# A hybrid encoder block: the first four MLP units in two token halves, and GpSimd scaling part of three tiles

## The chip, the cores and the metric

The kernel runs on one NeuronCore of a Trainium2 chip. The metric is the device time of one execution in microseconds (us); lower is better. Engines: TensorE (PE in the profile), VectorE (DVE), ScalarE (ACT), GpSimd (POOL), and SyncE (SP), which issues the weight loads.

## What is computed

512 tokens of width 2048 in float32: an adaLN-modulated token-mixing layer of two parallel attention groups, an output projection, a residual, then an adaLN-modulated squared-ReLU MLP of width 8192. The change sits at the seam between the two:

```python
o = o @ w_out[l]
x = x + gt_a * rms_norm(o, g_post_attn[l])
h = rms_norm(x, g_pre_mlp[l]) * (1.0 + sc_m) + sh_m
y = jnp.square(jax.nn.relu(h @ w_mlp_in[l])) @ w_mlp_out[l]
x = x + gt_m * rms_norm(y, g_post_mlp[l])
```

## The kernel before

All programs are written out by hand, one per engine; semaphores tie them together, and each engine runs its instructions strictly in the order written. Float32 products are made of three passes: every operand is split into a high part (rounded, fp32r) and a low part (the rest), and TensorE adds high x high, high x low and low x high. For a weight, ScalarE copies the landed block `raw` to `hi` (`split_hi`, 128x1024) and VectorE subtracts to get `lo` (`split_lo`). A *unit* is one such block of 256 rows of a weight matrix, a ring of four of them is in flight.

The 512 tokens are four tiles t = 0 to 3 of 128 on the partitions. The last column block of the output projection runs tile by tile, so that the tiles finish one after another (`b_tile`, `w_used`). For each tile:

- VectorE adds the two attention groups' parts (`sum_tile`, L1742) and gates them (`gate_tile`, L1747), ScalarE squares (`square_last`, L1086, into PSUM bank 2 or 3 as scratch, hence `row_done` before the MLP may use these banks), VectorE and ScalarE make the factor (`z_variance`, `root`), VectorE adds the residual in two halves of 1024 columns (`residual`, L1793, both inputs in SBUF).
- ScalarE squares the result in two halves (L1107); one tile later `x1_variance`, `root`, `x1_factor` (L1778) give the second norm's factor `rstd`, semaphore `x1_rstd`.
- The tile is scaled by it into `z_tok`: columns 0 to 511 (`xn_ready`) and 512 to 2047 (`xn_rest`), on ScalarE for tiles 0 to 2 (L1090) and on VectorE for tile 3 (L1813).

Then TensorE transposes z_tok in blocks of 128x128 (L2466): four blocks make column block k (0 to 15) of all 512 tokens in one PSUM bank. ScalarE and VectorE turn it into h2 = x*gsc_m + shf_m (printed as h_f, h_hi, h_lo, whose memory it shares): for even k ScalarE makes both the float32 and the high part (L1117, L1118), for odd k VectorE makes the float32 part (L1819) and ScalarE copies it to the high part (L1121); VectorE subtracts for the low part (L1824). `h2_mid`, `h2_hi_done` and `h2_ready` count these.

MLP unit j needs column blocks k = 2j and 2j+1 and is 24 matmuls of 512 columns. `first_columns` does unit 0, `up_block` units 1 to 7, with `before_first` putting the transposes of four more blocks ahead of units 1, 3 and 5. Splits of units 1 to 5 stand among the h2 instructions (`FIRST_AFTER`).

GpSimd does nothing at the seam: its last instructions ahead of it are the loads of bias rows, and then it waits to store the MLP's results.

Of the kernel before, what the change touches and what calls it, by code (L numbers as in the profile page):

```python
# [193 lines left out]
def build(nc, a, out, x1_dram, y_dram):  # L194
    with ExitStack() as ctx:
# [525 lines left out]
        def _(act):  # L721
# [369 lines left out]

            for t in range(NT):
# [11 lines left out]
                for half in range(2):  # L1104
                    act.wait_ge(x1_ready, 2 * t + half + 1)
                    cols = slice(half * HALF, (half + 1) * HALF)
                    nc.scalar.activation(z_tok[:, t, cols], x_res[:, t, cols], ACT.Square, accum_out=stat[:, t, 1 + half:2 + half]).then_inc(x1_sq, 1)  # L1107
                act.dma_start(x1_d[t], x_res[:, t, :]).then_inc(x1_saved, 16)
# [2 lines left out]
            for k in range(KD):
                if k % 2 == 0:
                    src, g, b = bank[4 + k % 4][:], gsc_m[:, k:k + 1], shf_m[:, k:k + 1]
                    act.wait_ge(xn_turned, k + 1)
                    if k >= 4:
                        act.wait_ge(h2_ready, k - 3)
                    nc.scalar.activation(h2_f32[k % 4][:], src, ACT.Identity, scale=g, bias=b)  # L1117
                    nc.scalar.activation(h2_hi[:, k, :], src, ACT.Identity, scale=g, bias=b).then_inc(h2_hi_done, 1)  # L1118
                else:
                    act.wait_ge(h2_mid, k // 2 + 1)  # L1120
                    nc.scalar.activation(h2_hi[:, k, :], h2_f32[k % 4][:], ACT.Copy).then_inc(h2_hi_done, 1)  # L1121
                for j in FIRST_AFTER.get(k, ()):
                    split_hi(*at_mlp(0, j))
# [109 lines left out]
        def _(dve):  # L1233
# [578 lines left out]
            for cols, ready in ((slice(0, COLS), xn_ready), (slice(COLS, D), xn_rest)):  # L1812
                ts(z_tok[:, NT - 1, cols], x_res[:, NT - 1, cols], rstd[:, NT - 1, 1:2], None, ALU.mult).then_inc(ready, 1)  # L1813
            for k in range(KD):
                if k % 2 == 0:

                    dve.wait_ge(xn_turned, k + 2)
                    k1 = k + 1
                    ts(h2_f32[k1 % 4][:], bank[4 + k1 % 4][:], gsc_m[:, k1:k1 + 1], shf_m[:, k1:k1 + 1],  # L1819
                       ALU.mult, ALU.add).then_inc(h2_mid, 1)  # L1820
                else:
                    dve.wait_ge(h2_mid, k // 2 + 1)
                dve.wait_ge(h2_hi_done, k + 1)
                tt(h2_lo[:, k, :], h2_f32[k % 4][:], h2_hi[:, k, :].bitcast(F32), ALU.subtract).then_inc(h2_ready, 1)  # L1824
                for j in FIRST_AFTER.get(k, ()):
                    split_lo(*at_mlp(0, j))
# [231 lines left out]
        def _(pe):  # L2058
# [406 lines left out]
            def turn_x1(k, t, out_bank):  # L2465
                return nc.tensor.transpose(out_bank[:, t * P:(t + 1) * P], z_tok[:, t, k * P:(k + 1) * P], ident[:])  # L2466

            pe.wait_ge(b_sum, 4 * NB)
            for t in range(NT):
                pe.wait_ge(xn_ready, t + 1)  # L2470
                for k in range(4):
                    ins = turn_x1(k, t, bank[4 + k])
                    if t == NT - 1:
                        ins.then_inc(xn_turned, 1)
            pe.wait_ge(row_done, 4 * NB)


            def first_columns():
# [3 lines left out]
                pe.wait_ge(raw_used, at_mlp(0, 0)[0].count(1, 1))
                pe.wait_ge(h2_hi_done, 1)
                for n in range(4):
                    mm(bank[n][:], hi[s][:, 0, n * P:(n + 1) * P], h2_hi[:, 0, :], start=True, stop=False)
                    mm(bank[n][:], lo[s][:, 0, n * P:(n + 1) * P], h2_hi[:, 0, :], start=False, stop=False)
                pe.wait_ge(h2_ready, 1)
                for n in range(4):
                    mm(bank[n][:], hi[s][:, 0, n * P:(n + 1) * P], h2_lo[:, 0, :], start=False, stop=False)
                pe.wait_ge(h2_ready, 2)  # L2490
                for n in range(4):
                    wh, wl = hi[s][:, 1, n * P:(n + 1) * P], lo[s][:, 1, n * P:(n + 1) * P]
                    mm(bank[n][:], wh, h2_hi[:, 1, :], start=False, stop=False)
                    mm(bank[n][:], wh, h2_lo[:, 1, :], start=False, stop=False)
                    ins = mm(bank[n][:], wl, h2_hi[:, 1, :], start=False, stop=False)
                ins.then_inc(w_used, 1)
# [30 lines left out]

            def before_first(j):


                if j in (1, 3, 5):
                    pe.wait_ge(h2_ready, 2 * j + 2)
                    pe.wait_ge(xn_rest, NT)
                    for k in range(2 * j + 2, 2 * j + 6):
                        for t in range(NT):
                            ins = turn_x1(k, t, bank[4 + k % 4])
                        ins.then_inc(xn_turned, 1)
                pe.wait_ge(h2_ready, 2 * j + 2)

            first_columns()  # L2540
            up_block(0, 0, before_first, range(1, UNITS_D))
            pe.wait_ge(h2_ready, KD)
# [206 lines left out]
```

## Time and profile before

| | us |
|---|---|
| median of 3 runs | 2118.05 (2114.66 to 2118.88) |
| the profiled execution's own time | 2119.17 |
| its span, first to last instruction | 2117.5 |
| TensorE busy | 2068.4 |
| VectorE, ScalarE, GpSimd busy | 1493.1, 844.1, 150.0 |

Times in the views are us from the span's start. In a timeline row stand start, duration, engine, line, operation, tiles written and read, and in brackets how long the engine was idle before it and what ended that.

### The profile page before, as it was taken

The numbers are of one execution on the slowest core, as the hardware profiler recorded it, in microseconds if no ns is written. First come the engines' busy times: TensorE is split into PE (matmuls) and PEld (weight loads), VectorE is DVE, ScalarE is ACT, GpSimd is POOL, SyncE is SP. The second block draws the span as 40 slices with busy tenths as digits, with TensorE's granted clock in tenths as the row PEclk, the third lists the DMA queues.
The fourth block names the chain that finished last, engine by engine and source line by source line (L and its number), as shares of the span: only waits on it lengthen the run. The fifth ranks groups of instructions, "written<-read, shape, count | busy, mean of one in ns | idle before, by whom it ended". The sixth has DMA issues, their size and how long they took to land.

```text
span 2117.5 us, 26317 instructions
## 1 busy us (share of the span) xinstructions
PE 2068.4 (98%) x9370; PEld 1710.2 (81%) x9370; DVE 1493.1 (71%) x1797; ACT 844.1 (40%) x1153; POOL 150.0 (7%) x159
## 2 busy tenths in 40 slices
PE   7999999999999989999999999999999999999998
PEld 6887888887788878888888888888788888888886
DVE  5876898788877776445544454434889888888866
ACT  4444322588733363233322332233333333333422
POOL 0000000038700000000000000012000000000000
PEclk9999999999999999999999999999999999999999
DMA  9986869600287736655665566666767456456442
GB/s 310 323 296 216 276 210 250 199 30 11 68 280 234 254 128 228 222 187 188 222 235 187 188 204 224 216 229 219 252 235 262 136 215 260 150 207 238 178 179 80
DMA packets 214353, 435.20 MB, mean 206 GB/s; under 512 B 30180, under 2 KB 69768, under 8 KB 205448
## 3 DMA queue, kind: packets, MB, share of 16 engines
q1 hardware_dynamic: 196136, 361.43, 50.8%
q0 software_dynamic: 16704, 67.11, 8.9%
q10 hardware_dynamic: 1440, 5.70, 0.7%
q8 instruction: 44, 0.72, 0.1%
q14 instruction: 29, 0.24, 0.0%
HBM read 367.09 MB, written 67.11 MB: 205 GB/s over the span
## 4 chain that ended last, share of the span: by engine, by line
PE 81%; DVE 6%; DMA 5%; issue 3%; ACT 3%; POOL 2%; SPq 0%; DVEq 0%; ACTq 0%; POOLq 0%
PE bank L2085 10%; PE bank L2087 10%; PE bank L2086 10%; PE bank L2523 7%; PE bank L2525 7%; PE bank L2524 7%; PE bank L2072 6%; PE bank L2074 6%; PE bank L2073 6%; DMA y_dram<-y_out 1%; DMA rows<-in_g_post_mlp 1%; PE bank L2574 1%; PE bank L2573 1%; PE bank L2572 1%; DMA w<-in_w_mlp_out 1%
## 5 line engine op out<-in xcount | busy, mean ns | idle before, releaser
L1241 DVE TENSOR_TENSOR lo<-raw,hi 128x1024 fp32r<-128x1024 f32 (+2 forms) x234 | 275.7, 1182 | 375.1 <-ACT hi L728 373.0
L728 ACT ACTIVATE hi<-raw 128x1024 fp32r<-128x1024 f32 (+2 forms) x236 | 239.5, 1023 | 655.4 <-PE bank L2087 410.9
L2085 PE MATMUL bank<-h_hi,hi 128*128 128x512 f32 x1016 | 396.0, 390 | 0.0
L2087 PE MATMUL bank<-h_hi,lo 128*128 128x512 f32 x1016 | 395.3, 389 | 0.0
L2086 PE MATMUL bank<-h_lo,hi 128*128 128x512 f32 x1016 | 395.3, 389 | 0.0
L2523 PE MATMUL bank<-hi,y_use 128*128 128x512 f32 x784 | 307.0, 392 | 7.3 <-DVE acc L1968 3.8
L2525 PE MATMUL bank<-hi,y_use 128*128 128x512 f32 x784 | 305.8, 390 | 0.0
L2524 PE MATMUL bank<-lo,y_use 128*128 128x512 f32 x784 | 305.7, 390 | 0.0
L1184 ACT ACTIVATE hi<-w 128x1024 fp32r<-128x1024 f32 x168 | 178.2, 1062 | 295.5 <-PE bank L2525 221.8
L1892 DVE TENSOR_TENSOR lo<-w,hi 128x1024 fp32r<-128x1024 f32 x168 | 204.7, 1223 | 37.5 <-ACT hi L1184 36.8
L2085 PEld LDWEIGHTS bank<-h_hi,hi 128*128 128x128 f32 x1016 | 190.7, 188 | 40.1 <-issue 0.7
L2087 PEld LDWEIGHTS bank<-h_hi,lo 128*128 128x128 f32 x1016 | 190.7, 188 | 39.7
L2086 PEld LDWEIGHTS bank<-h_lo,hi 128*128 128x128 f32 x1016 | 190.7, 188 | 39.5 <-issue 0.2
L2523 PEld LDWEIGHTS bank<-hi,y_use 128*128 128x128 f32 x784 | 147.5, 188 | 43.1 <-issue 12.7
L2525 PEld LDWEIGHTS bank<-hi,y_use 128*128 128x128 f32 x784 | 147.5, 188 | 30.8
L2524 PEld LDWEIGHTS bank<-lo,y_use 128*128 128x128 f32 x784 | 147.5, 188 | 30.3
L2072 PE MATMUL bank<-hi,h_hi 128*128 128x512 f32 x320 | 125.9, 394 | 1.4 <-ACT q_o L886 1.4
L2074 PE MATMUL bank<-hi,h_lo 128*128 128x512 f32 x320 | 124.7, 390 | 0.0
L2073 PE MATMUL bank<-lo,h_hi 128*128 128x512 f32 x320 | 124.5, 389 | 0.0
L1968 DVE TENSOR_TENSOR acc<-bank,acc 128x1024 f32<-128x1024 f32 x84 | 102.5, 1220 | 0.0
L2072 PE MATMUL bank<-hi,o_hi 128*128 128x512 f32 x224 | 89.3, 399 | 0.1
L2074 PE MATMUL bank<-hi,o_lo 128*128 128x512 f32 x224 | 88.0, 393 | 0.0
(318 smaller groups left out, 3124.9 us busy)
## 6 DMA issues: line engine op xcount, KB each, us to landing
raw<-in_w_ada SPq DMA_DIRECT2D x192, 512.0 KB, 5.1
raw<-in_w_mlp_in SPq DMA_DIRECT2D x128, 512.0 KB, 4.3
w<-in_w_mlp_out SPq DMA_DIRECT2D x128, 512.0 KB, 5.2
y_dram<-y_out POOLq DMA_DIRECT2D x32, 1792.0 KB, 7.8
y_use<-y_dram SPq DMA_DIRECT2D x53, 1024.0 KB, 8.8
raw<-in_w_in SPq DMA_DIRECT2D x32, 512.0 KB, 5.4
raw<-in_w_out SPq DMA_DIRECT2D x32, 512.0 KB, 4.7
raw<-in_w_in SPq DMA_DIRECT2D x48, 256.0 KB, 5.8
```

Source lines behind the costliest of these rows:

```text
L728: ins = nc.scalar.activation(dst, src, ACT.Copy)
L1241: ins = tt(dst, src, high.bitcast(F32), ALU.subtract)
L1892: tt(lo[w.slot()][:], weight(np, i, h)[:], hi[w.slot()][:].bitcast(F32), ALU.subtract).then_inc(dn_lo, 1)
L2072: mm(acc[t][:], xh, hi[s][:, q, :], start=first and q == 0, stop=False)
L2073: mm(acc[t][:], xh, lo[s][:, q, :], start=False, stop=False)
L2074: ins = mm(acc[t][:], xl, hi[s][:, q, :], start=False, stop=last and q == QROWS - 1)
L2085: mm(acc[n][:], wh, act_hi[:, k, :], start=first and q == 0, stop=False)
L2086: mm(acc[n][:], wh, act_lo[:, k, :], start=False, stop=False)
L2087: ins = mm(acc[n][:], wl, act_hi[:, k, :], start=False, stop=last and q == QROWS - 1)
L2523: mm(bank[b + m][:], yh, hi[s][:, q, :], start=j == 0, stop=False)
L2524: mm(bank[b + m][:], yh, lo[s][:, q, :], start=False, stop=False)
L2525: ins = mm(bank[b + m][:], yl, hi[s][:, q, :], start=False, stop=j == PAIRS - 1)
```

## The change

TensorE's first four MLP units are done in two passes, first on tokens 0 to 255 (tiles 0 and 1) and later on tokens 256 to 511, each with 24 matmuls of 256 columns. To that end column blocks k = 0 to 7 are turned and made into h2 in halves too: `TURNED` lists 24 pieces i: 0 to 7 are blocks 0 to 7 of the first half, 8 to 15 the same blocks of the second half, 16 to 23 blocks 8 to 15 whole. The first three pieces are transposed between the projection's last matmuls of tile 3, and the h2 instructions of the first pieces and the splits of units 0 to 3 are placed among the steps of tiles 2 and 3 on ScalarE and VectorE. The scaling of columns 512 to 2047 of tiles 0 to 2 goes from ScalarE to GpSimd.

```diff
+FIRST_K = KD // 2
+TURNED = [(k, half) for half in range(2) for k in range(FIRST_K)] + [(k, None) for k in range(FIRST_K, KD)]
...
+        def turned_at(i):
+            k, half = TURNED[i]
+            if half is None:
+                return k, slice(0, T), bank[4 + i % 4][:], h2_f32[i % 4][:]
+            cols = slice(half * HALF_T, (half + 1) * HALF_T)
+            return k, cols, bank[4 + i % 4][:, 0:HALF_T], h2_half[i % 4][:]
...
+            def h2_high(i):
+                k, cols, src, mid = turned_at(i)
+                dst, g, b = h2_hi[:, k, cols], gsc_m[:, k:k + 1], shf_m[:, k:k + 1]
+                if i % 2 == 0:
+                    act.wait_ge(xn_turned, i + 1)
...
+                    nc.scalar.activation(dst, src, ACT.Identity, scale=g, bias=b).then_inc(h2_hi_done, 1)
+                    nc.scalar.activation(mid, src, ACT.Identity, scale=g, bias=b).then_inc(h2_mid, 1)
+                else:
+                    act.wait_ge(h2_mid, i + 1)
+                    nc.scalar.activation(dst, mid, ACT.Copy).then_inc(h2_hi_done, 1)
             for t in range(NT):
                 square_last(t)
                 if t:
                     root(2 * t, t - 1, 1)
+                if t == 3:
+                    split_hi(*at_mlp(0, 1))
                 root(2 * t + 1, t, 0)
                 if t:
                     act.wait_ge(x1_rstd, t)
                     scale_x1(t - 1, slice(0, COLS), xn_ready)
-                    if t < NT - 1:
-                        scale_x1(t - 1, slice(COLS, D), xn_rest)
-                    else:
-                        split_hi(*at_mlp(0, 0))
...
+                if t == 2:
+                    split_hi(*at_mlp(0, 0))
+                if t == 3:
+                    h2_high(2)
+                    h2_high(3)
+                x1_square(t, 0)
+                if t == 2:
+                    h2_high(0)
+                x1_square(t, 1)
+                if t == 2:
+                    h2_high(1)
+            split_hi(*at_mlp(0, 2))
             root(2 * NT, NT - 1, 1)
-            scale_x1(NT - 2, slice(COLS, D), xn_rest)
...
+            def h2_two(i):
+                h2_middle(i + 1)
+                h2_low(i)
+                h2_low(i + 1)
             for t in range(NT):
                 if t < NT - 1:
                     dve.wait_ge(b_tile, t + 1)
                 else:
+                    split_lo(*at_mlp(0, 0))
+                    h2_two(0)
                     dve.wait_ge(w_used, MLP_W)
                 sum_tile(NB - 1, t)
                 gate_tile(NB - 1, t)
                 if t:
                     x1_variance(t - 1)
+                if t == NT - 1:
+                    split_lo(*at_mlp(0, 1))
                 z_variance(t)
                 if t:
                     x1_factor(t - 1)
+                if t == NT - 1:
+                    h2_two(2)
                 residual(t)
-            split_lo(*at_mlp(0, 0))
+            split_lo(*at_mlp(0, 2))
             x1_variance(NT - 1)
+            h2_two(4)
             x1_factor(NT - 1)
...
+                    if t == NT - 1 and j == 6:
+                        pe.wait_ge(xn_ready, 2)
+                        pe.wait_ge(b_sum, 4 * (NB - 1) + 3)
+                        for i in range(3):
+                            turn_x1(i)
...
+            def first_columns(half, j):
...
+                for q in range(QROWS):
+                    k = QROWS * j + q
+                    i = FIRST_K * half + k
+                    pe.wait_ge(h2_hi_done, i + 1)
+                    for n in range(4):
+                        mm(bank[n][:, cols], hi[s][:, q, n * P:(n + 1) * P], h2_hi[:, k, cols], start=k == 0 and half == 0, stop=False)
+                        mm(bank[n][:, cols], lo[s][:, q, n * P:(n + 1) * P], h2_hi[:, k, cols], start=False, stop=False)
+                    pe.wait_ge(h2_ready, i + 1)
+                    for n in range(4):
+                        ins = mm(bank[n][:, cols], hi[s][:, q, n * P:(n + 1) * P], h2_lo[:, k, cols], start=False, stop=False)
...
+            pe.wait_ge(row_done, 4 * NB)
+            first_columns(0, 0)
+            pe.wait_ge(b_sum, 4 * NB)
+            turn_more(3, 4, 5)
+            first_columns(0, 1)
+            turn_more(6, 7)
+            first_columns(0, 2)
+            first_columns(0, 3)
+            turn_more(8, 9, 10, 11)
+            for j in range(FIRST_K // QROWS):
+                first_columns(1, j)
+                turn_more(12 + 2 * j, 13 + 2 * j)
+            up_block(0, 0, before_first, range(FIRST_K // QROWS, UNITS_D))
...
+            for t in range(NT - 1):
+                pool.wait_ge(x1_rstd, t + 1)
+                nc.gpsimd.tensor_scalar(z_tok[:, t, COLS:D], x_res[:, t, COLS:D], rstd[:, t, 1:2], None, ALU.mult).then_inc(xn_rest, 1)
```

`turn_more` transposes the pieces it is given, with the waits that free their banks. How the orders move at two places:

VectorE from the residual of tile 2 to that of tile 3, before (L1793 is the residual, L1742 and L1747 sum and gate of tile 3):

```order
L1793 SCALAR_TENSOR_TENSOR x_res<-z_tok,rstd,x_res 128x1024 x2
L1742 SCALAR_TENSOR_TENSOR part<-bank,r_out,part 128x512
L1747 TENSOR_TENSOR z_tok<-part,comb 128x512
L1772 TENSOR_TENSOR stat<-stat 128x1
L1773 TENSOR_SCALAR stat_v<-stat 128x1
L1783 TENSOR_REDUCE stat<-row_sq 128x1
L1784 TENSOR_SCALAR stat_v<-stat 128x1
L1778 RECIPROCAL rstd<-stat_s 128x1
L1789 RECIPROCAL rstd<-stat_s 128x1
L1793 SCALAR_TENSOR_TENSOR x_res<-z_tok,rstd,x_res 128x1024 x2
```

The same place after (L1827 is the residual, L1776 the sum, L1275 `split_lo`, L1836 `h2_middle`, L1843 `h2_low`), first from the residual of tile 2 to the gate of tile 3:

```order
L1827 SCALAR_TENSOR_TENSOR x_res<-z_tok,rstd,x_res 128x1024 x2
L1275 TENSOR_TENSOR lo_85<-raw_73,hi_81 128x1024
L1836 TENSOR_SCALAR h_half_164<-bank,gsc_m,shf_m 128x256
L1843 TENSOR_TENSOR h_lo<-h_half_163,h_hi 128x256
L1843 TENSOR_TENSOR h_lo<-h_half_164,h_hi 128x256
L1776 SCALAR_TENSOR_TENSOR part<-bank,r_out,part 128x512
L1781 TENSOR_TENSOR z_tok<-part,comb 128x512
```

and from there to the residual of tile 3:

```order
L1275 TENSOR_TENSOR lo_86<-raw_74,hi_82 128x1024
L1817 TENSOR_REDUCE stat<-row_sq 128x1
L1818 TENSOR_SCALAR stat_v<-stat 128x1
L1812 RECIPROCAL rstd<-stat_s 128x1
L1836 TENSOR_SCALAR h_half_166<-bank,gsc_m,shf_m 128x256
L1843 TENSOR_TENSOR h_lo<-h_half_165,h_hi 128x256
L1843 TENSOR_TENSOR h_lo<-h_half_166,h_hi 128x256
L1823 RECIPROCAL rstd<-stat_s 128x1
L1827 SCALAR_TENSOR_TENSOR x_res<-z_tok,rstd,x_res 128x1024 x2
```

Four instructions have moved ahead of tile 3's sum, and four more stand between its gate and its residual.

ScalarE behind `square_last` of tile 3 up to the first h2 piece of unit 2's columns, after (L739 `split_hi`, L1088 `root`, L1101 the scaling, L1107 the squares of tile 3, L1121, L1122 and L1125 `h2_high`):

```order
L1088 ACTIVATE stat_s<-stat_v 128x1
L739 ACTIVATE hi_82<-raw_74 128x1024
L1088 ACTIVATE stat_s<-stat_v 128x1
L1101 ACTIVATE z_tok<-x_res,rstd 128x512
L1121 ACTIVATE h_hi<-bank,shf_m,gsc_m 128x256
L1122 ACTIVATE h_half_165<-bank,shf_m,gsc_m 128x256
L1125 ACTIVATE h_hi<-h_half_166 128x256
L1107 ACTIVATE z_tok,stat<-x_res 128x1024 x2
L1109 DMA x_dram<-x_res 128x2048
L739 ACTIVATE hi_83<-raw_75 128x1024
L1088 ACTIVATE stat_s<-stat_v 128x1
L1121 ACTIVATE h_hi<-bank,shf_m,gsc_m 128x256
```

Before, only the two roots, one scaling and one `split_hi` stood between `square_last` and the squares of tile 3, and the h2 instructions all came behind. L1109 is the store of the tile, which both kernels have.

## Rows read from the trace of the kernel before

**Rows 1.** The page: engines' busy us (share of span), chain by engine.

```profile
PE 2068.4 (98%) x9370; PEld 1710.2 (81%) x9370; DVE 1493.1 (71%) x1797; ACT 844.1 (40%) x1153; POOL 150.0 (7%) x159
...
PE 81%; DVE 6%; DMA 5%; issue 3%; ACT 3%; POOL 2%; SPq 0%; DVEq 0%; ACTq 0%; POOLq 0%
```

**Rows 2.** Waits of TensorE: who for whom, us, times, longest.

```profile
PE bank L2466 <- DVE z_tok L1813: 3.9, 1, 3.9
...
PE bank L2485 <- ACT h_hi L1118: 1.1, 1, 1.1
PE bank L2466 <- DVE part L1742: 1.0, 1, 1.0
PE bank L2466 <- ACT z_tok L1090: 0.9, 1, 0.9
```

**Rows 3.** Timeline, TensorE, 757 to 778.

```profile
757.63 0.39 PE L2449 MATMUL bank<-lo,o_hi 128*128 128x512 f32 x1
757.86 0.39 PE L2450 MATMUL bank<-hi,o_lo 128*128 128x512 f32 x1
...
768.00 0.77 PE L2485 MATMUL bank<-h_hi,hi 128*128 128x512 f32 x1 [1.05 <-ACT h_hi L1118]
...
772.86 0.40 PE L2493 MATMUL bank<-h_hi,hi 128*128 128x512 f32 x1
...
775.61 1.91 PE L2466 MATMUL bank<-ident,z_tok 128*128 128x128 f32 x16
777.27 0.47 PE L2085 MATMUL bank<-h_hi,hi 128*128 128x512 f32 x1
```

**Rows 4.** Windows: us, PE busy, PEclk, DMA share, GB/s.

```profile
764.00:766.00 2.00, 0.17 (x1) 0.89 0.98 393
...
771.00:772.00 1.00, 1.00 (x4) 0.50 0.06 16
772.00:773.00 1.00, 1.00 (x5) 0.81 0.00 0
```

**Rows 5.** Timeline, VectorE, 758 to 764.

```profile
758.29 0.75 DVE L1742 SCALAR_TENSOR_TENSOR part<-bank,r_out,part 128x512 f32<-128x512 f32 x1 [0.46 <-PE bank L2450]
...
760.78 2.48 DVE L1793 SCALAR_TENSOR_TENSOR x_res<-z_tok,rstd,x_res 128x1024 f32<-128x1024 f32 x2
```

**Rows 6.** Timeline, TensorE at 739.94; then line L2087's weight loads.

```profile
739.94 1.84 PE L2459 MATMUL bank<-ones,mod_acc 128*128 128x1 f32 x16
...
L2087 PEld LDWEIGHTS bank<-h_hi,lo x1016: 187/188/188, 777.6 to 1474.9; 128*128 128x128 f32 x170
```

**Rows 7.** Groups of ScalarE and VectorE, 741 to 775, and L1843.

```profile
L1090 ACT ACTIVATE z_tok<-x_res,rstd 128x1536 f32<-128x1536 f32 x3 | 4.7, 1566 | 0.0
...
L1090 ACT ACTIVATE z_tok<-x_res,rstd 128x512 f32<-128x512 f32 x3 | 2.2, 724 | 0.0
...
L1824 DVE TENSOR_TENSOR h_lo<-h_f,h_hi 128x512 fp32r<-128x512 f32 x4 | 2.7, 688 | 0.6 <-ACT h_hi L1118 0.5 <-ACT h_hi L1121 0.2
...
L1843 DVE TENSOR_TENSOR y_mix<-y_mix x28: 424/426/426, 823.7 to 1396.7; 128x256 f32<-128x256 f32 x28
```

**Rows 8.** Groups of GpSimd by form: busy, mean ns, idle.

```profile
L2611 POOL TENSOR_TENSOR sq_sum<-sq_sum,sq 128x512 f32<-128x512 f32 x15 | 20.1, 1341 | 31.4 <-ACT sq L975 31.4
...
L2623 POOL CAST q_hi<-q_o 128x512 fp32r<-128x512 f32 x10 | 6.3, 630 | 281.9 <-PE bank L2306 281.9
...
L2648 POOL MEMSET sq_sum<- 128x1024 f32 x1 | 1.0, 957 | 7.1 <-PE bank L2366 7.1
```

**Rows 9.** Timeline, all engines, 549 to 551; then line L1629.

```profile
549.16 1.48 POOL L2611 TENSOR_TENSOR sq_sum<-sq_sum,sq 128x512 f32<-128x512 f32 x1
...
549.40 1.78 DVE L1629 TENSOR_TENSOR lo<-raw,hi 128x512 fp32r<-128x512 f32 x1
...
550.58 1.08 POOL L2643 CAST v_hi<-v_lat 128x512 fp32r<-128x512 f32 x1
...
L1629 DVE TENSOR_TENSOR lo<-raw,hi x4: 680/701/1785, 518.1 to 554.9; 128x512 fp32r<-128x512 f32 x4
```

More of the change, by code:

```diff
@@ L122 @@
 MLP_RAW_END = MLP_RAW_LAST + MLP_N
-FIRST_AFTER = {3: [1], 7: [2, 3], 11: [4, 5]}
 FIRST_SPLIT = 6
+FIRST_K = KD // 2
+TURNED = [(k, half) for half in range(2) for k in range(FIRST_K)] + [(k, None) for k in range(FIRST_K, KD)]
+TURNED_N = len(TURNED)
 PAIRS = FCH // 2
@@ L294, in build @@
         h2_f32 = [sb(f"h2_f32_{i}", 188 + 2 * i, [T]) for i in range(4)]
+        h2_half = [sb(f"h2_half_{i}", 188 + i, [HALF_T]) for i in range(4)]
         y_mix = sb("y_mix", 116, [SLOTS + 1, HALF_T])
@@ L1090, in scale_x1, with x1_square @@
                 nc.scalar.activation(z_tok[:, t, cols], x_res[:, t, cols], ACT.Copy, scale=rstd[:, t, 1:2]).then_inc(ready, 1)
+            def x1_square(t, half):
+                act.wait_ge(x1_ready, 2 * t + half + 1)
+                cols = slice(half * HALF, (half + 1) * HALF)
+                nc.scalar.activation(z_tok[:, t, cols], x_res[:, t, cols], ACT.Square, accum_out=stat[:, t, 1 + half:2 + half]).then_inc(x1_sq, 1)
+                if half:
+                    act.dma_start(x1_d[t], x_res[:, t, :]).then_inc(x1_saved, 16)
+            def h2_high(i):
[3 more added lines that the diff above has]
+                    act.wait_ge(xn_turned, i + 1)
+                    if i >= 2 * FIRST_K:
+                        act.wait_ge(h2_ready, max(2 * FIRST_K, i - 3))
+                    elif i >= 4:
+                        act.wait_ge(h2_ready, i - 3)
+                    nc.scalar.activation(dst, src, ACT.Identity, scale=g, bias=b).then_inc(h2_hi_done, 1)
[3 more added lines that the diff above has]
+                    nc.scalar.activation(dst, mid, ACT.Copy).then_inc(h2_hi_done, 1)
             for t in range(NT):
@@ L1099, in _ @@
                     scale_x1(t - 1, slice(0, COLS), xn_ready)
-                    if t < NT - 1:
-                        scale_x1(t - 1, slice(COLS, D), xn_rest)
-                    else:
-                        split_hi(*at_mlp(0, 0))
[L1104 to L1108, printed above, removed]
-            root(2 * NT, NT - 1, 1)
-            scale_x1(NT - 2, slice(COLS, D), xn_rest)
[L1111 to L1123, printed above, removed]
+                if t == 2:
[10 more added lines that the diff above has]
+            split_hi(*at_mlp(0, 2))
+            root(2 * NT, NT - 1, 1)
+            for i in range(4, 2 * FIRST_K):
+                h2_high(i)
+                if i == 5:
+                    split_hi(*at_mlp(0, 3))
+            for i in range(2 * FIRST_K, TURNED_N):
+                h2_high(i)
+                if i in (2 * FIRST_K + 1, 2 * FIRST_K + 5):
+                    split_hi(*at_mlp(0, 4 + (i - 2 * FIRST_K) // 4))
             def relu_pair(g, f, pr):
@@ L1793, in residual, with h2_middle, h2_low @@
                     stt(x_res[:, t, cols], z_tok[:, t, cols], rstd[:, t, 0:1], x_res[:, t, cols], ALU.mult, ALU.add).then_inc(x1_ready, 1)
+            def h2_middle(i):
+                k, _, src, mid = turned_at(i)
+                dve.wait_ge(xn_turned, i + 1)
+                if i >= 4:
+                    dve.wait_ge(h2_hi_done, i - 3)
+                dve.wait_ge(h2_mid, i)
+                ts(mid, src, gsc_m[:, k:k + 1], shf_m[:, k:k + 1], ALU.mult, ALU.add).then_inc(h2_mid, 1)
+            def h2_low(i):
+                k, cols, _, mid = turned_at(i)
+                dve.wait_ge(h2_mid, i + 1)
+                dve.wait_ge(h2_hi_done, i + 1)
+                tt(h2_lo[:, k, cols], mid, h2_hi[:, k, cols].bitcast(F32), ALU.subtract).then_inc(h2_ready, 1)
+            def h2_two(i):
+                h2_middle(i + 1)
+                h2_low(i)
+                h2_low(i + 1)
             for t in range(NT):
@@ L1806, in _ @@
                     x1_factor(t - 1)
+                if t == NT - 1:
+                    h2_two(2)
                 residual(t)
-            split_lo(*at_mlp(0, 0))
+            split_lo(*at_mlp(0, 2))
             x1_variance(NT - 1)
+            h2_two(4)
             x1_factor(NT - 1)
             dve.wait_ge(x1_rstd, NT)
[L1812 to L1826, printed above, removed]
+            ts(z_tok[:, NT - 1, 0:COLS], x_res[:, NT - 1, 0:COLS], rstd[:, NT - 1, 1:2], None, ALU.mult).then_inc(xn_ready, 1)
+            split_lo(*at_mlp(0, 3))
+            h2_two(6)
+            ts(z_tok[:, NT - 1, COLS:D], x_res[:, NT - 1, COLS:D], rstd[:, NT - 1, 1:2], None, ALU.mult).then_inc(xn_rest, 1)
+            for i in range(FIRST_K, TURNED_N, 2):
+                h2_two(i)
+                if i in (2 * FIRST_K, 2 * FIRST_K + 4):
+                    split_lo(*at_mlp(0, 4 + (i - 2 * FIRST_K) // 4))
             def mix_pair(g, f, pr):
@@ L2431, in out_block, with turn_x1 @@
                         spread_ga(n)
+            def turn_x1(i):
+                k, half = TURNED[i]
+                _, _, dst, _ = turned_at(i)
+                tiles = range(NT) if half is None else (2 * half, 2 * half + 1)
+                for m, t in enumerate(tiles):
+                    ins = nc.tensor.transpose(dst[:, m * P:(m + 1) * P], z_tok[:, t, k * P:(k + 1) * P], ident[:])
+                ins.then_inc(xn_turned, 1)
             out_block(0, first=True)
@@ L2463, in _ @@
             pe.wait_ge(mod_read, MODS + 4)
[L2465 to L2474, printed above, removed]
@@ L2475, in _ @@
-            pe.wait_ge(row_done, 4 * NB)
-            def first_columns():
-                w = at_mlp(0, 0)[1]
-                s = w.slot()
[L2482 to L2496, printed above, removed]
+            def first_columns(half, j):
+                r, w = at_mlp(0, j)
+                s = w.slot()
+                cols = slice(half * HALF_T, (half + 1) * HALF_T)
+                pe.wait_ge(raw_used, r.count(1, 1))
+                for q in range(QROWS):
[8 more added lines that the diff above has]
+                        ins = mm(bank[n][:, cols], hi[s][:, q, n * P:(n + 1) * P], h2_lo[:, k, cols], start=False, stop=False)
+                if half:
+                    ins.then_inc(w_used, 1)
@@ L2526, in dn_products, with turn_more @@
                         ins.then_inc(w_used, 1)
-            def before_first(j):
[L2531 to L2542, printed above, removed]
+            def turn_more(*which):
+                for i in which:
+                    if i == 4:
+                        pe.wait_ge(xn_rest, 2)
+                    if i == FIRST_K:
+                        pe.wait_ge(xn_ready, NT)
+                    if i == FIRST_K + 4:
+                        pe.wait_ge(xn_rest, NT)
+                    if i >= 4:
+                        pe.wait_ge(h2_ready, i - 3)
+                    turn_x1(i)
+            def before_first(j):
+                pe.wait_ge(h2_ready, FIRST_K + 2 * j + 2)
+                if j < UNITS_D - 2:
+                    turn_more(FIRST_K + 2 * j + 4, FIRST_K + 2 * j + 5)
+            pe.wait_ge(row_done, 4 * NB)
[11 more added lines that the diff above has]
+            up_block(0, 0, before_first, range(FIRST_K // QROWS, UNITS_D))
+            pe.wait_ge(h2_ready, TURNED_N)
             up_block(0, 1)
```

## The prediction

> **What bounds the kernel now.** The page first: TensorE (PE) is busy 98% of the span and holds 81% of the chain that ended last [rows 1]. So an edit on another engine pays only where TensorE waits. The list of its waits shows four at the seam between output projection and MLP: 3.9, 1.1, 1.0 and 0.9 us, 6.9 us together [rows 2]. The timeline places them: the last projection matmul starts at 757.86, the first MLP matmul at 768.00 [rows 3]; between them stand 16 transposes. The clock adds to that: after TensorE's idle stretch the granted clock falls in 764 to 766 from 1.00 (2.4 GHz) to 0.50 (1.2 GHz) and is back in 772 to 773 [rows 4]; twelve matmuls run from 768.00 to 772.86, 4.9 us, where the dense rate (starts 0.227 apart, 757.63 and 757.86 [rows 3]) gives 2.7. So 2.2 us go to the clock. From 777.27, where unit 1 starts, TensorE does not wait before the end of the first MLP half [rows 3]. What happens behind 777.27 is then a sum of TensorE work: whatever the change delays there is paid in full, as the rest of the up phase is dense.
>
> What is late at the seam is tile 3: VectorE's sum of tile 3 starts at 758.29 (L1742), its residual at 760.78 (L1793) and takes 2.48 for two halves [rows 5], then ScalarE squares, root, factor, z_tok, transposes, h2. That chain is serial.
>
> **The change, walked.** I put down for each engine its instructions in program order and let each start at the later of two times: the end of the one ahead of it, or 0.03 us after the last instruction that it waits for. Full-size durations are from rows; where instructions follow back to back I take the spacing of their starts in the timeline, which is some 0.08 less than a recorded duration. The same walk over the order of before puts unit 1 at 777.2 against 777.27 in the trace, so the method is good to about 0.3 us.
>
> New prices. *256-column matmul:* none in the trace. Half of 0.227 is 0.113; if the 0.0135 us by which 0.227 exceeds 512 columns at 2.4 GHz stays whole, it is 0.120. I take 0.120. A weight load is recorded as 0.188 [rows 6], and could be the floor; but sixteen one-column matmuls with their loads take 1.84 us, 0.105 apart [rows 6], so loads do overlap and I keep 0.188 as the upper bound only. *ScalarE on 256 columns:* 1024 columns fewer save 0.84 (1.566 against 0.724) [rows 7], so 256 fewer save 0.21: 0.45 from PSUM, 0.30 from SBUF. *VectorE on 256:* 0.42 against 0.69 for 512 [rows 7], starts 0.34 apart. *GpSimd on 1536 columns:* not in the trace. MEMSET of 1024 takes 0.96 and a CAST of 512 0.63 [rows 8]; CAST plus 1024 columns at MEMSET's rate is 1.6 at most, and MEMSET's rate over 1536 alone 1.4: 1.5, taken. CAST three times over gives 1.9; three two-input operations of 1.3 (L2611) give 3.9, the upper end.
>
> *GpSimd's new work holds VectorE.* At 549.40 a VectorE subtraction of 512 columns with both inputs in SBUF took 1.78 while GpSimd's L2611 ran from 549.16 to 550.64; its least is 0.68 [rows 9]. 1.78 is just the rest of GpSimd's instruction plus its own 0.6. The residual (z_tok and x_res) is such an instruction, and GpSimd's scaling of tile t is released by the very factor (x1_rstd) that stands 0.2 us ahead of the residual of tile t+1 on VectorE. So each scaling of 1.5 holds a residual by about 1.25, at tile 1 and at tile 2. The Trainium skill (GPSIMD Engine Reference, Key points) names the same sharing, for VectorE instructions with two SBUF inputs or in a 2-port mode; the trace agrees with 1.78 against 0.68. It speaks against this change: what ScalarE saves per tile (1.566, L1090 [rows 7]) lay beside the residual anyway.
>
> The walk, us from the span's start:
> - Residual 1, ready at 749.8, is held and ends 753.5; sum 2 follows at once; residual 2 is ready at 756.15, is held and ends 758.6.
> - Now VectorE does, ahead of sum 3, split_lo of unit 0, one middle and two lows of 256 columns, the last of which waits for ScalarE's square of tile 2 and copy: sum 3 starts at 762.5, before 758.29. 4.2 us late.
> - ScalarE's square_last(3) ends 763.85, so TensorE (row_done) starts its first half-matmuls at 764.0: 4.0 us *earlier* than before, after 5.3 us idle. This is the gain.
> - Before residual 3 stand split_lo of unit 1, factor 2, a middle and two lows, each pair handed over to ScalarE and back. Residual 3 runs 770.4 to 772.8; before 760.78 to 763.26. 9.6 us late.
> - Squares of tile 3 end 773.9, split_hi of unit 2 774.9, split_lo 776.2, root 776.7, h2 of k = 4 on ScalarE 777.2. TensorE, which ran dry at 772.6, starts unit 2's first half at 777.5. By then it has done 48 half-matmuls, the work of one whole unit, and 16 transposes.
>
> At that same time (777.27) before has done one whole unit and 32 transposes. So the early start buys nothing, and from here on the two are compared as sums:
> - start later: 777.5 against 777.3, +0.3 rounded up
> - 16 transposes more to do; sixteen take 1.66 from the start of the first to unit 1's start [rows 3]: +1.7
> - 144 half-matmuls still to come in place of 72 full ones: 144 x 0.120 - 72 x 0.227 = +0.95
> - clock: with about 5 us idle before 777.5, more than the 3.9 us wait in which it fell before [rows 2, 4], I expect 0.50 for some 4 us of work again, as from 768.00 to 772.4. Some 16 to 20 half-matmuls at 0.213 (256 columns at 1.2 GHz) instead of 0.120, part of it in waits anyway: +1.6. The half clock of before lies ahead of 777.27 and is in the comparison already; that of the first burst (764) hides behind the wait for tile 3.
> - new waits: h2 of k = 0 second half 0.1 and 0.4, split_lo of units 4 and 5 0.3 each: +1.1
>
> Sum +5.7 us. VectorE's own waits, the x1 stores and the POOL queue (its row loads are issued ahead of the scaling, and its first save waits for the first MLP half) lie beside TensorE work and cost nothing; units 6 to 8 are split 1 to 2 us later than before while TensorE needs them 5 later, so no weight is late. The profiled execution took 2119.17 with a span of 2117.5; the median of the runs is 2118.05, 1.1 lower, within their spread. A difference carries over: **2118.05 + 5.7 = 2123.7 us**, 0.27% slower. A measurement of this kernel tells about 0.2%, 4.2 us, from no change.
>
> The Trainium skill (TensorE: Matmul & The Clock Gate, Back-to-back issue gap) gives 262 cycles for 256 columns and 518 for 512, 109 and 216 ns at 2.4 GHz. The trace has 227 for 512, so the measurement decides. By the page's gap the sum would be 1.6 lower, +4.1.
>
> **Rivals.**
> 1. *No hold by GpSimd.* If its scaling fits between VectorE's instructions, or is done before the residual, both residuals keep their times: sum 3 starts at 760.4, TensorE at 761.9, unit 2 at 775.2, and the walk ends 2.3 (clock full) to 3.3 us later than before: about 2121, inside 0.2%. For it: GpSimd itself stretches too (a CAST took 1.08 at 550.58 [rows 9], beside VectorE, against its mean of 0.63), so the two may share. Against: 1.78.
> 2. *GpSimd at the two-input rate*, 3.9 us a tile: each residual held 3.65; the walk ends 10.8 later, 2128.9. For: its rate for a scalar from memory is not shown. Against: the one-input CAST.
> 3. *Weight load as floor.* With 0.13 per half-matmul +1.2 on the sum, with 0.15 +3.6, with 0.188 +8.4 (2132). Against: 0.105 apart.
> 4. *The second hole closes, and it is faster.* All rests on unit 2's first half starting when TensorE is free. If tile 3's residual kept its old place, as when VectorE takes sum 3 and residual 3 by 764 and the h2 halves are served in their gaps, TensorE would go from 762 without a stop: 48 half-matmuls 5.8 and 16 transposes 1.7 end at 769.5 instead of 777.5, no half clock behind. 5.7 - 8 - 1.6 = -3.9, 2114. It decides from unit 2 starting before 769. Against: in the program's order VectorE can't reach sum 3 before the low of the second h2 half, and residual 3 stands behind ScalarE's copy. Little chance.
> 5. *The change does not start TensorE early*: first half-matmul at 768 or later, e.g. a hold longer than I think. Then everything behind shifts by what it is over 764 less the slack of the burst; it falls in with 2.
>
> **How the numbers follow.** Main case 0.43, rival 1 0.28, rival 2 (with 5) 0.12, rival 3 0.08, rival 4 0.05, and 0.04 for an end within 0.2% that no case here has. The main case spreads from under 4.2 (half-matmuls at 0.113, a clock that is back sooner) to above 7. Of the main case's 0.43 I put 0.06 under 4.2. Slower 0.37 + 0.12 + 0.08 = 0.57, same 0.28 + 0.06 + 0.04 = 0.38, faster 0.05. The range 2117.5 to 2129.0 takes in rival 1 with room below and rival 2, and leaves out rival 4 and most of rival 3.
>
> **What would show it.** Right: first half-matmul at 762 to 764.5, residual halves of tiles 1 and 2 at 2.5 instead of 1.28 while GpSimd runs, residual 3 at 768 to 771, a TensorE wait of about 5 us ahead of unit 2, clock 0.50 after it, 256-column matmuls 0.11 to 0.12 apart. Wrong: no such wait, or residuals at 1.28, or half-matmuls 0.15 apart and more, or TensorE waiting later in the up phase for weights.

## The result and the profile after

The changed kernel takes **2131.11 us** (median of 5, 2128.32 to 2133.55), before in the same runs 2118.88 (2114.66 to 2119.55). The ratio is 1.0058, 95% interval 1.0047 to 1.0069: slower by 12.2 us at the medians. Forecast were 2123.7 and at most 2129.0. The direction held, the size did not.

The profiled execution took 2133.55 with a span of 2131.9, 14.4 over that of before. To see where these 14.4 lie I cut both traces at two events that both have: the start of the residual of tile 1 on VectorE, and the last matmul of the up phase on TensorE. In the kernel before these stand at 749.87 and 1475.15; I call the 725.28 between them *the stretch*. After, from the timelines of VectorE (cut at 753, so only the first of the two halves is in the row) and TensorE:

```profile
751.59 4.18 DVE L1827 SCALAR_TENSOR_TENSOR x_res<-z_tok,rstd,x_res 128x1024 f32<-128x1024 f32 x1
...
1487.61 0.39 PE L2143 MATMUL bank<-h_hi,lo 128*128 128x512 f32 x1
```

The stretch is now 736.02, **+10.7**. Ahead of it stand +1.7: in this execution the granted clock over 20 to 50 us was 0.77 (before's profile 0.89), and kernels made from either one (below) show one value or the other: 0.77 in e2, e3 and e7, 0.89 in e1, e4, e5, e6 and e8. So I take it for no effect of the change. Behind the stretch stand +1.9 (644.29 to the span's end against 642.35), of which 1.0 is a longer wait for the first weights of the down phase. What the change did is thus looked for in the stretch, and below every kernel is compared by it too. For comparison with before, 1.72 is to be taken off the times of after.

The waits of TensorE at the seam, in place of [rows 2]:

```profile
PE bank L2546 <- ACT bank L1097: 7.0, 1, 7.0
...
PE bank L2546 <- ACT h_hi L1121: 4.9, 1, 4.9
...
PE bank L2495 <- ACT z_tok L1101: 1.4, 1, 1.4
```

13.3 us where before had 6.9. The cause can be read from GpSimd and VectorE. GpSimd's timeline, and VectorE's, with the residuals of tiles 1 and 2:

```profile
751.41 4.17 POOL L2756 TENSOR_SCALAR z_tok<-x_res,rstd 128x1536 f32<-128x1536 f32 x1 [39.41 <-DVE rstd L1812]
759.31 4.16 POOL L2756 TENSOR_SCALAR z_tok<-x_res,rstd 128x1536 f32<-128x1536 f32 x1 [3.74 <-DVE rstd L1812]
772.14 4.17 POOL L2756 TENSOR_SCALAR z_tok<-x_res,rstd 128x1536 f32<-128x1536 f32 x1 [8.66 <-DVE rstd L1812]
```

```profile
751.59 5.38 DVE L1827 SCALAR_TENSOR_TENSOR x_res<-z_tok,rstd,x_res 128x1024 f32<-128x1024 f32 x2
756.89 0.74 DVE L1776 SCALAR_TENSOR_TENSOR part<-bank,r_out,part 128x512 f32<-128x512 f32 x1
...
759.62 5.26 DVE L1827 SCALAR_TENSOR_TENSOR x_res<-z_tok,rstd,x_res 128x1024 f32<-128x1024 f32 x2
764.80 1.21 DVE L1275 TENSOR_TENSOR lo<-raw,hi 128x1024 fp32r<-128x1024 f32 x1
...
767.56 0.74 DVE L1776 SCALAR_TENSOR_TENSOR part<-bank,r_out,part 128x512 f32<-128x512 f32 x1
```

The scaling takes 4.17 us, where 1.5 was forecast. The residuals take 5.38 and 5.26 in place of 2.48 [rows 5], and only the first half of each pair is long: 4.18 at tile 1. They are thus held by 2.9 and 2.8 us. Sum 3 (L1776) starts at 767.56. On TensorE that arrives as:

```profile
769.26 0.55 PE L2546 MATMUL bank<-h_hi,hi 128*128 128x256 f32 x1 [6.95 <-ACT bank L1097]
...
783.37 0.55 PE L2546 MATMUL bank<-h_hi,hi 128*128 128x256 f32 x1 [4.89 <-ACT h_hi L1121]
```

The windows around both waits (columns as in [rows 4]):

```profile
764.00:766.00 2.00, 0.00 (x0) 1.00 0.16 66
...
770.00:774.00 4.00, 4.00 (x21) 0.50 0.28 74
774.00:776.00 2.00, 2.00 (x19) 0.97 0.43 163
...
784.00:787.00 3.00, 3.00 (x16) 0.50 0.36 134
787.00:789.00 2.00, 2.00 (x16) 0.80 0.44 74
```

TensorE goes to half clock twice: after 7 idle us, and again after 4.9.

### The profile page after: what moved, and what is told of

Same layout as the page of the kernel before. It is cut to its first block, busy times and chain, and to the rows that moved or that the text cites. A ratio compares the mean times of both kernels' runs of the same rounds, so it can differ in the third digit from the quotient of the medians.

```text
span 2131.9 us, 26571 instructions
## 1 busy us (share of the span) xinstructions
PE 2073.4 (97%) x9466; PEld 1719.1 (81%) x9466; DVE 1499.8 (70%) x1809; ACT 843.4 (40%) x1162; POOL 162.7 (8%) x162
## 4 chain that ended last, share of the span: by engine, by line
PE 84%; DVE 6%; ACT 3%; issue 3%; DMA 2%; POOL 1%; SPq 0%; DVEq 0%; ACTq 0%; POOLq 0%
PE bank L2141 11%; PE bank L2142 11%; PE bank L2143 11%; PE bank L2579 7%; PE bank L2581 7%; PE bank L2580 7%; PE bank L2128 6%; PE bank L2129 6%; PE bank L2130 6%; PE bank L2647 1%; PE bank L2646 1%; PE bank L2648 1%; PE bank L2200 1%; PE bank L2202 1%; PE bank L2201 1%
## 5 line engine op out<-in xcount | busy, mean ns | idle before, releaser
L1275 DVE TENSOR_TENSOR lo<-raw,hi 128x1024 fp32r<-128x1024 f32 (+2 forms) x234 | 275.6, 1181 | 381.0 <-ACT hi L739 378.9
L739 ACT ACTIVATE hi<-raw 128x1024 fp32r<-128x1024 f32 (+2 forms) x236 | 239.8, 1023 | 658.4 <-PE bank L2143 411.5
L2141 PE MATMUL bank<-h_hi,hi 128*128 128x512 f32 x992 | 386.6, 390 | 0.5 <-DVE lo L1275 0.5
L2142 PE MATMUL bank<-h_lo,hi 128*128 128x512 f32 x992 | 385.9, 389 | 0.0
L2143 PE MATMUL bank<-h_hi,lo 128*128 128x512 f32 x992 | 385.9, 389 | 0.0
L2141 PEld LDWEIGHTS bank<-h_hi,hi 128*128 128x128 f32 x992 | 186.2, 188 | 39.9 <-DVE lo L1275 1.0
L2142 PEld LDWEIGHTS bank<-h_lo,hi 128*128 128x128 f32 x992 | 186.2, 188 | 38.8 <-issue 0.2
L2143 PEld LDWEIGHTS bank<-h_hi,lo 128*128 128x128 f32 x992 | 186.2, 188 | 38.7
L2129 PE MATMUL bank<-lo,o_hi 128*128 128x512 f32 x224 | 87.9, 393 | 0.0
```

Source lines behind the costliest of these rows:

```text
L739: ins = nc.scalar.activation(dst, src, ACT.Copy)
L1275: ins = tt(dst, src, high.bitcast(F32), ALU.subtract)
L2129: mm(acc[t][:], xh, lo[s][:, q, :], start=False, stop=False)
L2141: mm(acc[n][:], wh, act_hi[:, k, :], start=first and q == 0, stop=False)
L2142: mm(acc[n][:], wh, act_lo[:, k, :], start=False, stop=False)
L2143: ins = mm(acc[n][:], wl, act_hi[:, k, :], start=False, stop=last and q == QROWS - 1)
```

## The experiments

Two causes stood against each other at the start. **The hold:** GpSimd's instruction keeps VectorE from starting a residual, and that is more than half of the loss. **The halves:** the loss is in the new order and its extra small work, whoever scales. Each kernel is told with its median and ratio (95% interval), and with its stretch against the 725.28 of before. Runs of before beside e1 to e4 have the median 2118.79, beside e5 to e7 2119.2, beside e8 2119.15.

**e1_scale_on_act.** The halves stay; ScalarE scales the rest of tiles 0 to 2 again, in its idle places.

```
         if t == 1:
+            scale_x1(0, slice(COLS, D), xn_rest)
...
             split_hi(*at_mlp(0, 1))
+            scale_x1(1, slice(COLS, D), xn_rest)
...
             h2_high(3)
+            scale_x1(2, slice(COLS, D), xn_rest)
...
-    nc.gpsimd.tensor_scalar(z_tok[:, t, COLS:D], x_res[:, t, COLS:D], rstd[:, t, 1:2], None, ALU.mult)
```

> The changed kernel with one part undone: columns 512 to 2047 of tiles 0 to 2 are scaled on ScalarE again, in places where it idles in the changed kernel; GpSimd has no work at the seam. Theory A (GpSimd's 4.17 us instruction holds VectorE's residual): the residual halves of tiles 1 and 2 take 2.48 together again instead of 5.38 and 5.26, sum 3 comes 5 us earlier, and the kernel is 6 to 8 us faster than the changed one, 2123 to 2125 us, still 3 to 6 slower than the one before, since tile 3's chain stands behind h2 pieces and splits. Rival B (the loss is the late place of tile 3's chain and the half clock alone, the hold being covered by waits that come anyway): under 2 us faster than the changed one, about 2130.

2124.42 us, ratio 1.0027 (1.0018 to 1.0036), stretch +4.3. Its residual of tile 1, and its two TensorE starts:

```profile
749.71 2.48 DVE L1831 SCALAR_TENSOR_TENSOR x_res<-z_tok,rstd,x_res 128x1024 f32<-128x1024 f32 x2
```

```profile
762.07 0.51 PE L2550 MATMUL bank<-h_hi,hi 128*128 128x256 f32 x1 [3.29 <-ACT bank L1097]
...
775.52 0.36 PE L2550 MATMUL bank<-h_hi,hi 128*128 128x256 f32 x1 [4.89 <-ACT h_hi L1121]
```

The time is in the expected range. The hold is gone, and with it 6.5 of the stretch's 10.7. That is a little more than the two holds (5.7). The rest, 4.3, belongs to the halves and their order: the second wait is still 4.9 us.

**e2_before_gpsimd.** The other part alone: the kernel before, with only the rest scaling of tiles 0 to 2 moved to GpSimd.

```
-    scale_x1(t - 1, slice(COLS, D), xn_rest)
...
-scale_x1(NT - 2, slice(COLS, D), xn_rest)
...
+for t in range(NT - 1):
+    pool.wait_ge(x1_rstd, t + 1)
+    nc.gpsimd.tensor_scalar(z_tok[:, t, COLS:D], x_res[:, t, COLS:D], rstd[:, t, 1:2], None, ALU.mult).then_inc(xn_rest, 1)
```

> The kernel before with one part of the change alone: GpSimd scales columns 512 to 2047 of tiles 0 to 2, all else as before, full-width units. Theory A: the residuals of tiles 1 and 2 are held some 2.8 us each, sum 3 comes near 763 instead of 758.3, TensorE's wait grows by 5, and with a longer half clock the kernel is 5 to 7 us slower than before, 2124 to 2126. Rival B: within 1 us of before.

2127.73 us, ratio 1.0038 (1.0025 to 1.0051), stretch +8.5: more than expected. In this order the third scaling meets a residual as well (764.34 on GpSimd, 764.64 on VectorE), so three are held:

```profile
748.72 5.38 DVE L1790 SCALAR_TENSOR_TENSOR x_res<-z_tok,rstd,x_res 128x1024 f32<-128x1024 f32 x2
...
756.74 5.25 DVE L1790 SCALAR_TENSOR_TENSOR x_res<-z_tok,rstd,x_res 128x1024 f32<-128x1024 f32 x2
764.64 5.25 DVE L1790 SCALAR_TENSOR_TENSOR x_res<-z_tok,rstd,x_res 128x1024 f32<-128x1024 f32 x2
```

Counted from the start of residual 1, residual 3 ends 7.8 later than before, and the other 0.7 comes from a longer half clock behind it (from the first MLP matmul to unit 1's start 10.0 us, for 9.3). So GpSimd alone makes before slower, without any halves.

**e3_gpsimd_pieces.** The changed kernel, with each scaling of 1536 columns issued as three of 512.

```
-    nc.gpsimd.tensor_scalar(z_tok[:, t, COLS:D], x_res[:, t, COLS:D], ...).then_inc(xn_rest, 1)
+    for n in range(1, NB):
+        cols = slice(n * COLS, (n + 1) * COLS)
+        ins = nc.gpsimd.tensor_scalar(z_tok[:, t, cols], x_res[:, t, cols], rstd[:, t, 1:2], None, ALU.mult)
+    ins.then_inc(xn_rest, 1)
```

> The changed kernel with each of GpSimd's three instructions of 1536 columns cut into three of 512. Theory A, hold for the length of one instruction: a residual half waits for the piece under way only, about 1 us, the two halves of a tile take 3.5 to 4.5 us instead of 5.3, and the kernel is 2 to 4 us faster than the changed one, 2127 to 2129. Rival C (the two engines share SBUF bandwidth and VectorE is slowed in proportion to the bytes GpSimd moves): the same bytes cost the same, residuals 5.3, no change, 2131.

2125.38 us, ratio 1.0031 (1.002 to 1.0042), stretch +5.2. GpSimd works longer than before, and VectorE is held less:

```profile
750.92 4.83 POOL L2758 TENSOR_SCALAR z_tok<-x_res,rstd 128x512 f32<-128x512 f32 x3 [39.03 <-DVE rstd L1812]
756.66 5.88 POOL L2758 TENSOR_SCALAR z_tok<-x_res,rstd 128x512 f32<-128x512 f32 x3 [0.91 <-DVE rstd L1812]
```

```profile
751.11 3.21 DVE L1827 SCALAR_TENSOR_TENSOR x_res<-z_tok,rstd,x_res 128x1024 f32<-128x1024 f32 x2
756.96 3.09 DVE L1827 SCALAR_TENSOR_TENSOR x_res<-z_tok,rstd,x_res 128x1024 f32<-128x1024 f32 x2
```

The holds are 0.7 and 0.6, less than expected (3.5 to 4.5 for two halves), and the kernel is faster than the hold theory had put it (2127 to 2129). Both halves of residual 1 are held, each for a little: 1.58 and 1.71 in place of 1.28. So what counts here is not GpSimd's total time but how long one instruction of it is: VectorE gets its turn near the end of each.

**e4_keep_busy.** The changed kernel, with identity transposes in TensorE's two waits: 55 ahead of unit 0 and 44 ahead of the transposes of k = 6 and 7. It prices the clock.

```
+def keep_busy(n, b):
+    for _ in range(n):
+        nc.tensor.transpose(bank[b][:, 0:P], ident[:], ident[:])
...
+keep_busy(55, 0)
 pe.wait_ge(row_done, 4 * NB)
...
+pe.wait_ge(h2_ready, 3)
+keep_busy(44, 6)
 turn_more(6, 7)
```

> The changed kernel with TensorE doing 55 transposes of the identity in its first wait and 44 in its second, into PSUM space that is free then; nothing else differs. If the half clock behind the two waits costs what the sum says: granted clock 1.00 throughout, the burst at 783 runs at 0.12 per half-matmul from its start, the kernel is 2 to 3 us faster than the changed one, about 2129 (the first burst's half clock being hidden behind tile 3's chain). If the half clock costs nothing because waits end it all: no change. If the added transposes are themselves in the way: slower.

2127.92 us, ratio 1.0049 (1.0035 to 1.0062), stretch +9.4. That is 1.3 less than after in the stretch, and 3.1 less by the medians, each against its own before; the expected 2 to 3 us are in the time and not in the stretch. The granted clock is 1.00 in every window of the seam:

```profile
784.00:787.00 3.00, 2.79 (x23) 1.00 0.28 46
```

Behind unit 2's start the stretch is 1.1 shorter (703.14 for 704.24). Ahead of it next to nothing is gained, though the transposes behind unit 0 come 2.3 sooner. VectorE's float32 part of piece 3 starts 0.9 sooner (22.26 after residual 1's start, for 23.19), but the two lows behind it now meet GpSimd's third scaling (770.51 to 774.67):

```profile
772.21 0.54 DVE L1836 TENSOR_SCALAR h_half<-bank,gsc_m,shf_m 128x256 f32<-128x256 f32 x1 [1.79 <-ACT h_half L1122]
772.67 1.74 DVE L1843 TENSOR_TENSOR h_lo<-h_half,h_hi 128x256 fp32r<-128x256 f32 x2
```

They end at 774.4, where ScalarE's copy for the second one is done by 773.2. So e4 prices the clock behind unit 2, and the clock ahead of it only mixed with a new hold. Most of the loss stands without the half clock.

**e5_reordered.** What is left after e1 should be the lateness of tile 3. This kernel has the halves, no GpSimd work, and another order of steps on two engines. VectorE's piece around tile 3 (S sum and gate, X and F variance and factor of x, Z variance of z, R residual, s split, w a pair of middles and lows; e1's order above):

```
-s0 w0 S3 X2 s1 Z3 F2 w2 R3 s2 X3 w4 F3
+s0 S3 X2 w0 Z3 s1 s2 w2 R3 w4 F2 s3 w6 X3 F3
```

And ScalarE's, from the squares of tile 2 to those of tile 3 (x square of the residual's half, h step of h2, q square of the row, rb and ra roots, s split, c and C scaling of the first 512 and of the rest):

```
-x20 h0 x21 h1 q3 rb2 s1 C1 ra3 c2 h2 h3 C2 x30 x31
+x20 h0 x21 s1 q3 h1 s2 h2 C1 rb2 ra3 h3 h4 s3 x30 h5 h6 x31
```

> The changed kernel with the halves kept, the rest scaling on ScalarE (no GpSimd work here) and the steps of ScalarE and VectorE written in another order: the sum of tile 3 goes ahead of the middles and lows of pair 0, and pairs 2, 4 and the splits of units 1, 2 go around residual 3, ahead of variance and factor 3. Theory: what is left after the hold (e1's +5.6) is that tile 3's chain is late and that TensorE runs dry in unit 2 (e1: 4.9 us, second half clock). By a sum over the steps with durations of the traces, residual 3 starts about 766 (e1: 768.6), the first matmul of unit 2 at about 769 (e1: 775.5), no wait over 2 us behind it and hardly a half clock: about 2114, range 2112 to 2118, so the halves would be a gain once the order fits them. Rival (the halves themselves cost it, by their 16 extra turns, one-column pairs and twice as many small instructions): 2120 to 2124.

2115.92 us, ratio 0.9986 (0.9978 to 0.9995), stretch **-2.9**, as expected. The second wait is gone; one wait of the seam is over 0.3 us:

```profile
PE bank L2508 <- ACT bank L1097: 2.6, 1, 2.6
```

```profile
761.13 0.35 PE L2508 MATMUL bank<-h_hi,hi 128*128 128x256 f32 x1 [2.59 <-ACT bank L1097]
...
769.45 0.36 PE L2508 MATMUL bank<-h_hi,hi 128*128 128x256 f32 x1
```

The halves add no transposes: 64 in both kernels, only more of them behind unit 2's start. The 0.120 for each half-matmul is still there. So "the halves themselves cost it" falls; in e1 and after they cost because tile 3 comes late. Whether a new order alone would also speed up the kernel before was not run.

**e6_reordered_gpsimd.** e5 with the scaling on GpSimd again, nothing else.

> e5 with the rest scaling of tiles 0 to 2 on GpSimd again, as in the change. Theory (VectorE's residual is held by GpSimd's 4.2 us instruction, some 2.8 us each time, on the path to tile 3's sum): residuals 1 and 2 take about 5.3 us for two, unit 0 starts about 4 to 5 us later than in e5, 2121 to 2125, 7 to 10 us over e5. Rival (the order covers the hold, since no other work waits for VectorE there): within 2 us of e5.

2127.13 us, ratio 1.0038 (1.0026 to 1.005), stretch +5.3, so 8.2 over e5 (11.2 at the medians) and above the expected 2121 to 2125. Residual 3 starts 5.8 later than in e5, counted from residual 1. Beside the two held residuals, the third scaling now falls on the lows of the h2 pairs:

```profile
778.03 5.06 POOL L2718 TENSOR_SCALAR z_tok<-x_res,rstd 128x1536 f32<-128x1536 f32 x1 [16.11 <-DVE rstd L1789]
```

```profile
777.85 1.21 DVE L1252 TENSOR_TENSOR lo<-raw,hi 128x1024 fp32r<-128x1024 f32 x1
778.97 0.54 DVE L1813 TENSOR_SCALAR h_half<-bank,gsc_m,shf_m 128x256 f32<-128x256 f32 x1
779.42 3.40 DVE L1820 TENSOR_TENSOR h_lo<-h_half,h_hi 128x256 fp32r<-128x256 f32 x2
```

These rows are the clearest on the mechanism. While GpSimd runs, VectorE's middle (the float32 part, one input, in PSUM) takes its usual 0.54, and the two lows with both inputs in SBUF take 3.40 in place of two times 0.42. The `split_lo` that was under way when GpSimd started has both inputs in SBUF too and takes its usual 1.21: what is under way is not held.

**e7_before_keep_busy.** The kernel before, 32 identity transposes ahead of tile 3's transposes and 7 ahead of unit 0.

> The kernel before with 32 identity transposes ahead of tile 3's transposes and 7 ahead of unit 0, in TensorE's waits of 3.9 and 1.1 us; nothing else is changed. It prices the clock at this place in the kernel before, where 765.6 to 772.4 ran at half. Theory: the granted clock stays 1.00 and the 20 or so 512-column matmuls and 4 transposes after the wait run at full rate: 1.5 to 2.5 us faster, 2116.5 to 2117.5. Rival (those matmuls are paced by the pairs' middles and lows on VectorE and ScalarE): within 0.7 us of before.

2118.94 us, ratio 1.0 (0.9991 to 1.001), stretch -2.0. The clock stays at 1.00 and the stretch is shorter by what was expected, but the time shows no gain. The profiled execution began its stretch 1.9 later than before's did, and its clock over the first 50 us was 0.86 against 0.93. The interval ends at -1.9, so a gain of 2 is neither shown nor well excluded.

**e8_reordered_busy.** e5 with 22 identity transposes in its one wait.

```
+keep_busy(22, 0)
 pe.wait_ge(row_done, 4 * NB)
 first_columns(0, 0)
```

> e5 with 22 identity transposes into a free bank in TensorE's one wait left there (2.6 us ahead of unit 0), behind which 761 to 765 ran at half clock. Theory: the granted clock stays 1.00 and the two units' first half-matmuls save about 1.3 us at the seam (32 of them at 0.120 and not 0.213 us, less what the transposes run over), so 0.5 to 2 us under e5, 2114 to 2115.5 by the median. Rival: unit 0 and 1 are paced by the pairs' middles and lows as soon as TensorE is faster, within 0.3 us of e5 at the seam.

2115.64 us, ratio 0.998 (0.9971 to 0.9989), stretch **-4.5**, so 1.6 less than e5. The windows in place of e5's 0.50:

```profile
762.00:764.00 2.00, 2.00 (x20) 1.00 0.50 187
764.00:766.00 2.00, 1.72 (x16) 1.00 0.76 185
```

Its median is the lowest of all: 3.5 us under before in its runs and some 15 under the change. It is just above the expected 2114 to 2115.5. e5 and e8 can't be told apart by time (0.3 at the medians); the stretch, from one execution of each, is what differs.

## Why the prediction came out as it did

- **The mechanism was named rightly, and the size of one term was not.** GpSimd's scaling holds the residuals of tiles 1 and 2. e1 takes the hold away and it goes, e2 has it without the rest of the change, and e6 puts it back. The Trainium skill (GPSIMD Engine Reference, Key points) names sharing of SBUF interfaces for VectorE instructions with two SBUF inputs; the trace of e6 agrees, 3.40 for two lows beside an unheld 0.54 from PSUM.
- **The failed term is "GpSimd on 1536 columns: 1.5, taken".** It measured 4.17. I took it from a MEMSET, which reads nothing, and a CAST; the nearer row was the two-input one (1.34 for 512 columns [rows 8], three times 4.0), which I had put down as the upper end with 0.12. The Trainium skill (GPSIMD Engine Reference, section Engine selection) calls one-input work on GpSimd roughly line-rate; here it takes 4.17 where VectorE takes 1.01 for the same form, and the measurement decides.
- **From it "hold 1.25 each" became 2.9 and 2.8**, 3.2 more over two tiles. Sum 3 came at 765.8 (767.56 less 1.72) for 762.5, the first half-matmul at 767.5 for 764.0, residual 3 at 774.7 for 770.4, unit 2 at 781.65 for 777.5. "Start later +0.3" is +4.4: 3.2 of the 4.1 between them are the holds.
- **The half clock of the first burst was not hidden.** The prediction let it cost nothing, behind the wait for tile 3. But residual 3 itself stands behind the float32 part of piece 3, and that waits for transposes which TensorE does only after unit 0, at half clock:

```profile
774.78 0.55 DVE L1836 TENSOR_SCALAR h_half<-bank,gsc_m,shf_m 128x256 f32<-128x256 f32 x1 [2.73 <-PE bank L2495]
```

  From unit 0's start to residual 3 it took 7.15, for 6.4 in the walk. In e4, at full clock, this row comes 0.9 sooner.
- **The other terms.** Transposes +1.7: 48 of 128 columns follow unit 2's start, for 32, as said. Halves +0.95: the starts of 256-column matmuls at full clock are 0.120 apart. Clock +1.6: from 783.37 to 787.77 twenty of them ran at 0.213, 1.9; with the clock full in e4, 1.1 of it comes back. Waits +1.1: about 1.8 with gaps, which was not measured but is what 10.7 less 4.4, 1.7, 0.95 and 1.9 leaves. The sum behind unit 2's start was forecast as 5.35 and measured 6.4.
- **Rival 1's walk (no hold) was right in its places.** It had TensorE at 761.9 and unit 2 at 775.2, and e1 shows 762.07 and 775.52. Its end, +2.3 to +3.3, measured +4.3 in the stretch, and +5.6 by the medians.
- **Rival 2 (two-input rate, +10.8) hit the stretch's +10.7, in part by luck.** Its duration of 3.9 was near. But it had VectorE wait to GpSimd's recorded end, 3.65; the hold was 2.9. Two times 0.8 too much there made up for what the walk lacked behind unit 2 and in e1's part.
- **Rival 4 (the second hole closes, 2114, deciding at unit 2 before 769) is e5 in all but the scaling**, with unit 2 at 769.45 and 2115.92. The order and GpSimd keep the change from it; nothing in the halves does.
- **Rival 3 (weight load as floor) is out**: the half-matmuls start 0.120 apart. Its additions fit some 120 of them, not the 144 of the sum, with which they would be 1.4, 4.3 and 9.8.
- **Not told apart:** the medians lie above before's by more than the stretch does, by 1.5 for after (12.2 for 10.7), 1.3 for e1, 1.4 for e3, 2.6 for e6, 1.7 for e7 and 1.0 for e8, and by less than 0.5 either way for e2, e4 and e5. Part of it is the profiled executions' own start, and part the first wait of the down phase, which reads 2.5 before, 3.5 after, 5.3 in e1 and 2.1 in e4. It doesn't follow the change, and I have no cause for it.

## What to carry to other kernels

Before moving elementwise work from a half idle ScalarE to GpSimd, look at what VectorE does at that moment: the price was not GpSimd's time but up to 2.9 us whenever a VectorE instruction with two SBUF inputs came up while it ran, and work that already lay beside something (ScalarE's 1.57) saved nothing by moving. If GpSimd must do it, cut it into short instructions (holds of 0.7 for 2.9). When TensorE starts early on half the data, check the serial chain of the *last* tile: the early start paid only once the sum and residual of tile 3 stood ahead of the new small steps in VectorE's order.
